# Output projection of the delta rule begins with the first eight heads' channels, turned ahead of the last outputs; weight slots laid out anew

## The reference, cut to what matters

```
_, y = lax.scan(step, S0, ...)                       # 16 heads, 256 tokens
mean = y.mean(-1, keepdims=True)                     # per token and head, over 64 channels
var = jnp.square(y - mean).mean(-1, keepdims=True)
y = ((y - mean) * lax.rsqrt(var + GN_EPS)).reshape(B, T, C) * gn_g + gn_b
y = y + bonus
h = (y * g) @ w_o                                    # 1024 x 1024
x = layer_norm(ALPHA * x + h, ...)
```

## Time and profile before

| what | value |
|---|---|
| median of three runs | 1507.2 us |
| the profiled execution | 1507.1 us, its span (first to last instruction) 1505.2 us |
| TensorE busy, of the span | 1403.7 us, 93% |
| VectorE, ScalarE, GpSimd busy | 59%, 42%, 5% |
| mean granted TensorE clock | 0.974 of full |
| last outputs of the delta rule begin | 338.42 us |
| transposes of the layer norm's result begin | 381.14 us |

### The profile page before, as it was taken

The page is one execution under the profiler, slowest core; times in us unless marked ns, Lnnn a source line. Parts: engine busy times, 40 slices in busy tenths (PEclk is TensorE's granted clock), DMA queues, the critical chain, the costliest instruction groups (busy, mean ns, idle before and its releaser), DMA issues.

```text
span 1505.2 us, 21641 instructions
## 1 busy us (share of the span) xinstructions
PE 1403.7 (93%) x9280; PEld 1256.9 (84%) x9280; DVE 883.4 (59%) x1292; ACT 630.7 (42%) x899; POOL 78.5 (5%) x43
## 2 busy tenths in 40 slices
PE   7989899997899999999999999899988888699998
PEld 4676898996899997876789999898988887599997
DVE  5168435426744547555564545798998756465555
ACT  1343342434443345444444344533434544544443
POOL 0011030001200002100110000100000000000000
PEclk9999999998999999999999999998999999999999
DMA  9422000005565553623175555644543434255550
GB/s 287 145 74 112 1 1 1 1 1 196 168 196 181 183 189 116 227 88 109 35 244 191 175 195 168 192 132 141 167 140 126 155 112 156 68 183 181 185 193 28
DMA packets 154383, 204.96 MB, mean 136 GB/s; under 512 B 7440, under 2 KB 128400, under 8 KB 154160
## 3 DMA queue, kind: packets, MB, share of 16 engines
q1 hardware_dynamic: 154288, 203.59, 41.3%
HBM read 202.53 MB, written 1.05 MB: 135 GB/s over the span
## 4 chain that ended last, share of the span: by engine, by line
PE 72%; DVE 20%; ACT 5%; issue 1%; DMA 0%; SPq 0%; DVEq 0%; ACTq 0%
PE PS L464 17%; PE PS L465 17%; PE PS L466 17%; DVE PH L1999 6%; DVE WL L1561 4%; PE PS L765 3%; PE PS L752 3%; PE PS L769 2%; PE PS L668 2%; DVE AL L1588 2%; PE PS L613 1%; PE PS L718 1%; DVE PA L1812 1%; ACT WH L1098 1%; PE PS L633 1%
## 5 line engine op out<-in xcount | busy, mean ns | idle before, releaser
L1561 DVE TENSOR_TENSOR WL<-RG,WH 128x2048 fp32r<-128x2048 f32 x163 | 372.4, 2291 | 218.4 <-ACT WH L1098 218.4
L464 PE MATMUL PS<-AH,WH 128*128 128x256 f32 x1664 | 481.1, 289 | 17.6 <-DVE AL L1588 13.8
L465 PE MATMUL PS<-AL,WH 128*128 128x256 f32 x1664 | 476.2, 286 | 0.0
L466 PE MATMUL PS<-AH,WL 128*128 128x256 f32 x1664 | 475.7, 286 | 0.0
L1098 ACT ACTIVATE WH<-RG 128x2048 fp32r<-128x2048 f32 x164 | 311.3, 1906 | 95.8 <-PE PS L466 95.7
L464 PEld LDWEIGHTS PS<-AH,WH 128*128 128x128 f32 x1664 | 324.5, 195 | 24.6 <-issue 12.8
L465 PEld LDWEIGHTS PS<-AL,WH 128*128 128x128 f32 x1664 | 324.9, 195 | 1.7 <-issue 0.2
L466 PEld LDWEIGHTS PS<-AH,WL 128*128 128x128 f32 x1664 | 324.7, 195 | 0.0
L464 PE MATMUL PS<-WH,HH 128*128 128x512 f32 x304 | 118.8, 391 | 0.1
L465 PE MATMUL PS<-WL,HH 128*128 128x512 f32 x304 | 118.7, 390 | 0.0
L466 PE MATMUL PS<-WH,HL 128*128 128x512 f32 x304 | 118.3, 389 | 0.0
(11 more groups left out here) (269 smaller groups left out, 1779.7 us busy)
## 6 DMA issues: line engine op xcount, KB each, us to landing
RG<-in_ffn_w_in SPq DMA_DIRECT2D x44, 1024.0 KB, 5.2
RG<-in_w_ff SPq DMA_DIRECT2D x32, 1024.0 KB, 5.4
RG<-in_w_in SPq DMA_DIRECT2D x30, 1024.0 KB, 5.2
RG<-in_ffn_w_down SPq DMA_DIRECT2D x22, 1024.0 KB, 4.9
RG<-in_w_rkv SPq DMA_DIRECT2D x12, 1024.0 KB, 5.5
RG<-in_moba_w_qkv SPq DMA_DIRECT2D x12, 1024.0 KB, 5.3
RG<-in_w_o SPq DMA_DIRECT2D x4, 1024.0 KB, 9.0
RG<-in_wx_kv SPq DMA_DIRECT2D x4, 1024.0 KB, 5.8
```

Of the source, the lines that this page charges most:

```text
L464: e.matmul(o, lh, rh, start=start, stop=False)
L465: e.matmul(o, lh, rl, start=False, stop=False)
L466: return e.matmul(o, ll, rh, start=False, stop=stop)
L1561: v.tensor_tensor(WL[:, lo_n % NW, :], ring(SPLIT[lo_n]), WH[:, lo_n % NW, :].bitcast(F32), ALU.subtract).then_inc(s_lo, 1)
```

## The change

Four things are changed.

1. **Memory.** `WH` and `WL` become one tensor `WW` of six slots; the slots of the three pieces in turn are 2/3, 0/1 and 4/5 (high/low). `BT`, `KTt`, `RR` and `SS` move to `KX` and `VX`, `SA` to the end of `PA`. So the slots of `wo0` (columns 8192 to 12287) are free during the second inversion; those of `wo1` lie over `AT` of groups 2 and 3, those of `wo2` over `GT_` and `BV`.
2. **Order of the weights.** `wo0`, `wo1` are now the first 512 rows of `w_o` (first and last columns), `wo2`, `wo3` the last 512 rows.
3. **Transposes and projection.** `turn_y(0)` turns the first eight heads' channels (both chunks) before `outputs(1, 1)`; `y_out(0)`, `y_odd(0)` and `y_low(0)` split them. Four token pieces with `wo0`, `wo1` need no more than that. `turn_y(1)` stands behind three of them.
4. **Splits.** The split of `wo0` moves into levels 4 (ScalarE) and 5 (VectorE) of the second inversion, GpSimd makes none, that of `wo1` moves ahead of `gn_square(4)` and between steps 1 and 2 of unit 4, that of `wo2` behind unit 4.

```diff
+        WW = ctx.enter_context(nc.sbuf_tensor("WW", [128, 2 * NW, 2048], F32R))
+        WH = [WW[:, n, :] for n in (2, 0, 4)]
+        WL = [WW[:, n, :] for n in (3, 1, 5)]
...
+        SA = PA[:, NLOW + 12808:NLOW + 13832].rearrange("p (g n) -> p g n", g=4)
...
-                piece(f'wo{n}', wcols(a['w_o'], 512 * (n // 2), 512, 4 * (n % 2), 4))
+                piece(f'wo{n}', wcols(a['w_o'], 512 * (n % 2), 512, 4 * (n // 2), 4))
...
+            def turn_y(part):
+
+                for tt in range(2):
+                    e.wait_ge(s_yn, 2 * part + tt + 1)
+                    for k in range(4 * part, 4 * part + 4):
+                        o_ = PS[k // 2][:, (2 * (k % 2) + tt) * 128:(2 * (k % 2) + tt + 1) * 128]
+                        t = e.transpose(o_, YY[:, tt, k * 128:(k + 1) * 128], ident)
+                        if tt and k % 2:
+                            t.then_inc(s_tr, 1)
...
+                else:
+                    turn_y(0)
                 outputs(half, 1)
...
-            to_chan('y', YY, [0, 1, 2, 3])
-            token(('wo0', 'wo1'), (4, 6), ready=H_AT['y'])
-            token_last(('wo2', 'wo3'), (5, 7))
+            split_ready('wo0')
+            token_piece('wo0', 4, 0, 0, ready=H_AT['y'])
+            token_piece('wo0', 6, 1, 0)
+            split_ready('wo1')
+            token_piece('wo1', 5, 0, 0)
+            e.wait_ge(s_yy, 8)
+            turn_y(1)
+            token_piece('wo1', 7, 1, 0)
+            split_ready('wo2')
+            token_piece('wo2', 4, 0, 1, ready=H_AT['y'])
+            split_ready('wo3')
+            token_piece('wo3', 5, 0, 1)
+            token_piece('wo2', 6, 1, 1)
+            token_piece('wo3', 7, 1, 1)
...
+            def y_out(part):
+                s.wait_ge(s_tr, 2 * part + 1)
+                for m in range(2):
+                    t = s.activation(XT[:, 4 * part + m, :], PS[2 * part][:, m * 256:(m + 1) * 256], ACT.Copy, bias=0.0, scale=1.0)
+                t.then_inc(s_tca, 1)
+                for c in (2 * part, 2 * part + 1):
+                    s.wait_ge(s_tcv if c % 2 else s_tca, part + 1)
+                    sl = slice(c * 512, c * 512 + 512)
+                    s.activation(AH[:, sl], Xb[:, sl], ACT.Copy, bias=0.0, scale=1.0).then_inc(s_th, 1)
...
+                    if half == 1 and l == 4:
+                        ahead('wo0', 0)
...
+                    y_out(0)
                 outputs(half, 1)
-            ahead('wo0', 0)
+            ahead('wo0', 1)
             gn_square(4, 1, 1)
             gn_sqrt(4, 1, 1)
-
-            chan_out('y', XT, [0, 1, 2, 3])
-            ahead('wo0')
+            s.wait_ge(s_yn, 4)
+            ahead('wo0', 2)
+            y_out(1)
             ahead('wo1')
...
+                    if half == 1 and l == 5:
+                        ahead('wo0', 0)
...
-            for step in range(8):
+            y_odd(0)
+            y_low(0)
+            group_norm(4, 1, 1, 0)
+            group_norm(4, 1, 1, 1)
+            ahead('wo0', 1)
+            for step in range(2, 8):
                 group_norm(4, 1, 1, step)
-
-            chan_out('y', XT, [0, 1, 2, 3])
-            ahead('wo0')
+            y_odd(1)
+            ahead('wo0', 2)
+            y_low(1)
             ahead('wo1')
-            ln_token(0, 1, 'wo1', 'wo3')
+            ln_token(0, 1, 'wo2', 'wo3')
...
-            g.wait_ge(s_hi, 1)
-            g.tensor_tensor(WL[:, 0, :], ring('wo0'), WH[:, 0, :].bitcast(F32), ALU.subtract).then_inc(s_lo, 1)
```

More of the change, by code:

```diff
@@ L155, in build @@
         AL = ctx.enter_context(nc.sbuf_tensor("AL", [128, 2048], F32R))
-        WH = ctx.enter_context(nc.sbuf_tensor("WH", [128, NW, 2048], F32R))
-        WL = ctx.enter_context(nc.sbuf_tensor("WL", [128, NW, 2048], F32R))
+        WW = ctx.enter_context(nc.sbuf_tensor("WW", [128, 2 * NW, 2048], F32R))
+        WH = [WW[:, n, :] for n in (2, 0, 4)]
+        WL = [WW[:, n, :] for n in (3, 1, 5)]
         with nc.sbuf_tensor("PF", [128, 2048], F32) as PF, nc.sbuf_tensor("HH", [128, 2, 512], F32R) as HH, \
@@ L261, in build @@
         AT = take(8192).rearrange("p (i s t) -> p i s t", i=16, s=4)
[L262 to L266, removed]
+        BT = KX[:, 0:2, :].rearrange("p a t -> p (a t)").rearrange("p (m n) -> p m n", m=4)
+        KTt = KX[:, 2:4, :].rearrange("p a t -> p (a t)").rearrange("p (m n) -> p m n", m=4)
+        RR = VX[:, 0, :].rearrange("p (g n) -> p g n", g=2)
+        SS = VX[:, 1, :].rearrange("p (m e n) -> p m e n", m=4, e=2)
+        SA = PA[:, NLOW + 12808:NLOW + 13832].rearrange("p (g n) -> p g n", g=4)
         GT_ = PA[:, 12288:14336].rearrange("p (t c) -> p t c", t=2)
@@ L476, in wsl @@
             s = W[name] % NW
-            return v3(WH[:, s, :], n)[:, k, c0:c1], v3(WL[:, s, :], n)[:, k, c0:c1]
+            return v3(WH[s], n)[:, k, c0:c1], v3(WL[s], n)[:, k, c0:c1]
         def tensor_program(e):
@@ L547, in to_chan @@
                         mem_unit(between)
-                    if name == 'y':
-                        e.wait_ge(s_yn, (3, 4)[tt])
-                    elif name in ('ln0', 'ln1', 'ln2'):
+                    if name in ('ln0', 'ln1', 'ln2'):
                         q = int(name[2])
@@ L558, in to_chan @@
                     for k in range(8):
-                        if (name, tt, k) == ('y', 0, 4):
-                            e.wait_ge(s_yy, 8)
                         o_ = PS[banks[k // 2]][:, (2 * (k % 2) + tt) * 128:(2 * (k % 2) + tt + 1) * 128]
@@ L1097, in ahead @@
                         s.wait_ge(s_wdone, hi_n - NW + 1)
-                    s.activation(WH[:, hi_n % NW, :], ring(SPLIT[hi_n]), ACT.Copy, bias=0.0, scale=1.0).then_inc(s_hi, 1)
+                    s.activation(WH[hi_n % NW], ring(SPLIT[hi_n]), ACT.Copy, bias=0.0, scale=1.0).then_inc(s_hi, 1)
                     hi_n += 1
@@ L1551, in vector_program @@
             own_dve = Own(v, s_vo)
-            lo_n = 1
+            lo_n = 0
             def ahead(name, n=2):
@@ L1558, in ahead @@
                     v.wait_ge(s_hi, lo_n + 1)
-                    if lo_n == 1:
-                        v.wait_ge(s_lo, 1)
-                    v.tensor_tensor(WL[:, lo_n % NW, :], ring(SPLIT[lo_n]), WH[:, lo_n % NW, :].bitcast(F32), ALU.subtract).then_inc(s_lo, 1)
+                    v.tensor_tensor(WL[lo_n % NW], ring(SPLIT[lo_n]), WH[lo_n % NW].bitcast(F32), ALU.subtract).then_inc(s_lo, 1)
                     lo_n += 1
@@ L1565, in piece_done, with y_odd, y_low @@
                 v.wait_ge(s_wdone, W[name] + 1)
+            def y_odd(part):
+                v.wait_ge(s_tr, 2 * part + 2)
+                for m in range(2):
+                    t = v.tensor_copy(XT[:, 4 * part + 2 + m, :], PS[2 * part + 1][:, m * 256:(m + 1) * 256])
+                t.then_inc(s_tcv, 1)
+            def y_low(part):
+                for c in (2 * part, 2 * part + 1):
+                    sl = slice(c * 512, c * 512 + 512)
+                    v.wait_ge(s_th, H_AT['y'] + c + 1)
+                    v.tensor_tensor(AL[:, sl], Xb[:, sl], AH[:, sl].bitcast(F32), ALU.subtract).then_inc(s_tl, 1)
             def chan_out(name, dst, banks):
```

## The result

The change makes the kernel faster. The changed kernel took 1493.51 us (median of six runs, 1490.96 to 1494.8), the kernel before 1504.74 us in six runs (1500.69 to 1508.62); the ratio on record is 0.9916, 95% interval 0.9897 to 0.9934 (the quotient of the two medians is 0.9925). So the gain is 10 to 13 us; 11.8 us had been forecast, a ratio of 0.9922.

What follows compares the result with a forecast made beforehand. TensorE bounds, with an 8.47 us gap ending the delta rule. Gap 8.47, wait 0.95, low clock 3.7 and tails 0.6, less new waits 1.6 + 0.3, give 11.8 off 1507.1: 1495.3, forecast 1495.4 us, range 1493.0 to 1500.0.

Steps and rivals of the forecast that it cites:

- The stage: From the last outputs of the delta rule to the norm's transposes: shrinks from 42.72 to 30.9 us, by 11.8 us.
- the shift was handed through the norm: Layer norm behind the projection: waits tile for tile as before, so the 11.8 us gain passes on whole.
- The new wait: TensorE before the projection's fifth piece: waits 1.6 us for VectorE's remainder of the second half's first chunk.
- the 0.15 us before the sixth piece: Late in the projection: the low part of wo3, made by VectorE, costs TensorE 0.15 us more.
- The stall: Unit 4's 8-element VectorE instruction: held 3.2 us by GpSimd's split of wo0; rival that GpSimd was not the cause: 0.04.
- The clock: Behind the 8.47 us gap: 14 matmuls and eight transposes at half clock, 3.7 us to be given back.
- The rival of a drop behind the new wait: Projection's fifth piece: clock falls to half after TensorE's 1.6 us wait, costing 2.8 us, 1498.2 us; chance 0.10.
- The product starts early: Projection's first product at about 344.7 instead of 356.52; rival that it starts only with unit 4: 1506.3 us, chance 0.03.
- Nothing was given back at the start of the feed-forward layer: Rival there: loads or norm's end tied to something else, up to all the gain lost, 1507.2 us; chance 0.03.
- The projection never ran at half clock: Rival in the projection: 96 matmuls at half clock cost 19.2 us more, 1514.6 us; chance 0.03.
- the cover for the split of wo0: Second inversion, levels 4 and 5: idle ScalarE and VectorE time hides the split; without it at most 4.2 us.
- the no-wait case: Rival before the projection's fifth piece: no wait there, 1.9 us more saved, 1493.5 us; chance 0.05.

Runs made afterwards that it cites:

- e6: The changed kernel, unedited, run and profiled again: ratio 0.9935 to the kernel before, stage 30.9 us.
- e2: Changed kernel with early transposes, weight order and later splits undone; memory layout and wo0 split in the inversion kept, none on GpSimd: ratio 0.997, stage 39.5 us.
- e3: Changed kernel with the low part of wo1 made by GpSimd instead of VectorE: ratio 0.9937 to the kernel before, stage 32.4 us.
- e1: Kernel before, with 36 unused matmuls between the first and second eight transposes of y: ratio 0.9973, stage 40.9 us.
- e0: The kernel before, unedited, run and profiled again: ratio 0.9999, single runs 1503.86 to 1508.49 us.
- e4: Changed kernel with the split of wo0 taken out of the second inversion and made behind the last outputs: ratio 0.9988 to the kernel before, stage 38.1 us.
- e7: Changed kernel with GpSimd's residual work at the first norm held until VectorE's last remainder of that norm's result: ratio 0.9917 to the kernel before.

## Why the prediction was right, and where it was wrong

**The stage.** Right step by step, as far as this profile and e6's tell. Forecast and measured, brought to the start of the early transposes (338.42 in the prediction, 338.06 in the profile): first product 6.3 and 6.35 us behind it, end of unit 4 14.7 and 14.6, wait before the fifth piece 1.6 and 1.23, norm's transposes 30.9 and 30.7. The third piece did not wait, the clock stayed at 1.00, and the shift was handed through the norm. The new wait is 0.4 us smaller than the sum of three rows in series, and the 0.15 us before the sixth piece did not show.

**The stall.** The 3.2 us were put down to GpSimd from one pair of end times. That was an inference; e2 (the stall is gone with GpSimd's instruction) and e3 (it is back with another) show that it was right.

**The clock.** Its price in the kernel before was set at 3.7 us. As a part of the 42.7 us of that execution it is right; as a thing of its own it is not: e1 got 1.9 us for it, and e0 shows the same stage at 41.6 us because the clock came back sooner. The rival of a drop behind the new wait did not come true at 1.23 us, nor at 1.38 and 1.13 (e3), but did at 4.72 (e4). For waits between these two sizes the profiles show both outcomes (see "The range").

**The rivals.** None of them came true in the change. The product starts early; e4 shows what it takes to delay it. Nothing was given back at the start of the feed-forward layer: its second wait ends at 381.61 instead of 393.98, 12.4 us earlier, as the transposes of the norm's result are (368.79 instead of 381.14). The projection never ran at half clock. The largest condition is one that I had passed over in a line, the cover for the split of wo0: I priced its loss at 4.2 us of inversion, but where the split has to stand instead it costs 7.3 us.

**The range.** This is the step that failed: the level from which the 11.8 us were taken, and the width around it. The sum was "1507.1 - 11.8 = 1495.3", and the low end "from below the no-wait case, by the 0.2 us of the new places and 0.3 of reading, 1493.0". Both took one profiled execution, and the three runs beside it, as the level of everything outside the stage, and gave its variation no term. Six runs of the kernel before have their median at 1504.74 us, 2.5 us below the 1507.2 of the first three; 1504.74 - 11.8 is 1492.9, below the low end with the gain exactly as forecast. The prediction also called any distance from the norm's transposes to the end other than 1124.1 us a sign that it was wrong. It is 1120.4 us in the change, but 1123.4 in e0, 1120.2 in e1 and 1122.8 in e6, so the sign says nothing about the change: that distance was not fixed to begin with.

The kernel before ran between 1500.69 and 1508.62 us in its first six runs, and the same 7001 entries behind the stage took 1120.2 to 1126.8 us. From the rows above: in the first profile of the kernel before, TensorE was busy 1055.8 of 1124.1 us and idle 68.3; in that of the change 1057.0 of 1120.4 and idle 63.4. What differs is how much work falls into stretches of half clock and how long TensorE waits; both change from run to run. One place in two profiles of the kernel before, first its first profile, then e0:

```profile
1237.82 0.47 PE L464 MATMUL PS<-WH,AH 128*128 128x512 f32 x1 [3.06 <-DVE AL L1594]
```

```profile
1235.46 0.77 PE L464 MATMUL PS<-WH,AH 128*128 128x512 f32 x1 [3.06 <-DVE AL L1594]
```

The same product stands behind the same wait of 3.06 us. The granted clock of the 3.2 us that follow is 1.00 in the first and 0.50 in e0. At another place it is the other way round: behind a wait of 3.44 us at 600.7 it is 0.59 for 3.3 us in the first profile, and 1.00 behind one of 3.42 in e0. A term of 2 or 3 us to each side would have held the result. Why the clock falls at such a place in one run and not in another stays open: no experiment moved the low stretches outside the stage on purpose.

## What to carry to other kernels

Fill a gap on the bounding engine with the part of the next product whose operands are ready, and look first at which memory keeps those operands from being ready: here moving small tiles off the weight slots is what permitted the early split, on which 7.3 of the 12.0 us hang. Before work is given to GpSimd, look at what VectorE does on the critical path at that time; before it is taken away in time (e7), at what waits for GpSimd's end. Sum a change from its own stage, but take the level and the width of the range from several runs, for they hold all that lies outside that stage.

## What the runs showed of the hardware

- Some instructions of GpSimd and VectorE shut each other out for their whole length, in both directions. An 8-element VectorE instruction took 3.33 to 3.42 us and ended within 0.05 us of GpSimd's of 4.5 us (before, e3). In e7 GpSimd's 128x1024 product took 4.46 us beside VectorE's splits, 2.36 to 2.42 us where it had started ahead of them (the change, e7), and three splits took 12.2 instead of 6.8 us. The Trainium skill, SBUF — State Buffer, "SBUF: two separate sides", calls it an exclusive lock; these rows agree. Not every instruction is shut out. GpSimd's split of wo0 ran from 346.30 to 350.80, and this reduction inside that time took the 0.69 us of the earlier trace rows:

```profile
346.77 0.69 DVE L1873 TENSOR_REDUCE ST<-PA 128x8 f32<-128x512 f32 x1 [0.70 <-ACT PA L1289]
```

- In the stage, TensorE's granted clock was at half behind waits of 4.72 to 8.47 us (before, e0, e2, e4), and at full behind a single one of 1.0 to 1.6 us (the change, e1, e3, e4, e6). Behind one of 3.06 us at the same place of the same kernel it was at full in one profile and at half in the other. How long it then stayed low differed too: behind the gap of 8.47 us, 3.4 us of the product in e0 and 6.0 us in the first profile.
- Useless matmuls in a gap of 8.47 us kept the clock up and made the kernel faster, 0.9973.
